# Two step orders of a two-layer mixture-of-experts kernel: MLA preparation steps in attention, and the last pair of experts

## The reference, cut to what matters

```
q_a = (rms_norm(q_lat, q_norm) @ w_uq).reshape(b, t, H_A, NOPE_A + ROPE_A)   # 8 heads, 64 + 32
kv  = (ckv @ w_ukv).reshape(b, t, H_A, NOPE_A + V_A)                         # keys 64, values 64
k   = concatenate([kv[..., :NOPE_A], broadcast(kpe)])
out = concatenate([o_mla, o_gqa]) @ w_out
```

```
hid = silu(einsum("nd,edf->nef", x, w_gate)) * einsum("nd,edf->nef", x, w_up)
y   = einsum("nef,efd->nd", hid * gates[:, :, None], w_down)
x   = layer_norm(ALPHA * x + mod_gate * y)
```

## Time and profile before

| what | before |
|---|---|
| median of 3 runs | 821.88 us (820.93 to 823.96) |
| the profiled execution's own time | 821.88 us |
| its span, first to last instruction | 820.1 us |
| TensorE matmuls busy | 759.0 us, 93% |
| VectorE, ScalarE, GpSimd busy | 237.2, 150.9, 59.7 us |
| read from memory | 278.99 MB, mean 350 GB/s |
| mean granted TensorE clock | 0.977 |

### The profile page before, as it was taken

The page is one execution under the profiler, slowest core; times in us unless marked ns, Lnnn a source line. Parts: engine busy times, 40 slices in busy tenths (PEclk is TensorE's granted clock), DMA queues, the critical chain, the costliest instruction groups (busy, mean ns, idle before and its releaser), DMA issues.

```text
span 820.1 us, 9612 instructions
## 1 busy us (share of the span) xinstructions
PE 759.0 (93%) x3769; PEld 361.2 (44%) x3769; DVE 237.2 (29%) x550; ACT 150.9 (18%) x390; POOL 59.7 (7%) x116
## 2 busy tenths in 40 slices
PE   4799799999999999997999999999999999997894
PEld 1345444556544443443334564455544434442431
DVE  0002634447401101000418227374601010010417
ACT  0110312325011110111112132233211101110200
POOL 0000000000100010101000110000100002101000
PEclk9599999999999999999999999999999999999998
DMA  8999999915399999999999999752299999999981
GB/s 305 390 304 396 390 390 416 415 68 206 121 418 417 419 421 417 419 416 415 421 401 374 389 380 423 299 211 104 109 419 416 422 417 416 421 418 416 418 352 52
DMA packets 78530, 287.46 MB, mean 351 GB/s; under 512 B 6508, under 2 KB 12140, under 8 KB 62100
## 3 DMA queue, kind: packets, MB, share of 16 engines
q1 hardware_dynamic: 74452, 275.60, 84.9%
q10 hardware_dynamic: 2880, 7.03, 2.2%
q0 software_dynamic: 1152, 4.19, 1.3%
HBM read 278.99 MB, written 7.82 MB: 350 GB/s over the span
## 4 chain that ended last, share of the span: by engine, by line
PE 56%; SPq 23%; DMA 9%; DVE 8%; ACT 3%; issue 2%; POOL 0%; DVEq 0%; ACTq 0%
PE bank L1094 13%; SPq L600 12%; PE bank L1128 7%; DMA ring<-in_exp_w_down 6%; SPq L595 6%; PE bank L932 6%; PE bank L789 5%; PE bank L769 4%; SPq L596 4%; PE bank L1065 3%; DMA ring<-in_w_mod 2%; PE bank L878 2%; PE bank L671 2%; PE bank L720 2%; PE bank L820 2%
## 5 line engine op out<-in xcount | busy, mean ns | idle before, releaser
L1094 PE MATMUL bank<-ring,arena 128*64 128x512 f32 x1024 | 227.6, 600 | 11.3 <-DMA ring<-in_exp_w_up 10.5
L1094 PEld LDWEIGHTS bank<-ring,arena 128*64 128x64 f32 x1024 | 75.2, 138 | 160.3 <-issue 148.8
L1128 PE MATMUL bank<-ring,arena 128*64 128x512 f32 x512 | 114.3, 596 | 6.0 <-DMA ring<-in_exp_w_down 4.9
L1679 DVE TENSOR_TENSOR arena<-bank,arena 128x256 f32<-128x256 f32 x32 | 13.6, 424 | 231.5 <-ACT arena L1848 231.5
L1128 PEld LDWEIGHTS bank<-ring,arena 128*64 128x64 f32 x512 | 35.8, 137 | 72.7 <-issue 63.6
L1065 PE MATMUL bank<-arena 128*128 128x128 f32 x512 | 62.1, 275 | 0.0
L1065 PEld LDWEIGHTS bank<-arena 128*128 128x128 f32 x512 | 59.7, 192 | 1.0 <-issue 0.5
L1758 ACT ACTIVATE arena<-bank 128x512 f32<-128x512 f32 (+6 forms) x67 | 37.2, 579 | 107.6 <-PE bank L789 34.0
L1848 ACT ACTIVATE arena<-bank 128x256 f32<-128x256 f32 x32 | 12.3, 383 | 225.7 <-PE bank L1094 225.7
L1695 DVE COPY arena<-bank 128x512 f32<-128x512 f32 x14 | 9.7, 691 | 118.7 <-PE bank L1128 118.7
L789 PE MATMUL bank<-ring,arena 128*128 128x256 f32 (+1 forms) x128 | 41.6, 486 | 0.0
(11 more groups left out here) (182 smaller groups left out, 679.6 us busy)
## 6 DMA issues: line engine op xcount, KB each, us to landing
ring<-in_exp_w_gate SPq DMA_DIRECT2D x64, 1024.0 KB, 19.8
ring<-in_exp_w_up SPq DMA_DIRECT2D x64, 1024.0 KB, 19.6
ring<-in_exp_w_down SPq DMA_DIRECT2D x64, 1024.0 KB, 23.7
ring<-in_w_mod SPq DMA_DIRECT2D x24, 2048.0 KB, 19.8
expert_rows<-arena ACTq DMA_DIRECT2D x12, 512.0 KB, 7.9
ring<-in_w_out_ab SPq DMA_DIRECT2D x2, 2048.0 KB, 19.2
ring<-in_w_in_c SPq DMA_DIRECT2D x2, 2048.0 KB, 23.2
ring<-in_w_out_c SPq DMA_DIRECT2D x2, 2048.0 KB, 12.0
```

The source lines that it names most:

```text
L1094: mm = nc.tensor.matmul(pb(key)[SLOTS * hf:SLOTS * (hf + 1), :], xeT[b][:, k * P + SLOTS * a:k * P + SLOTS * (a + 1)], w[:, :, k % 4, hf * ...
L1128: mm = nc.tensor.matmul(pb(key)[SLOTS * a:SLOTS * (a + 1), :], hp[:, c:c + SLOTS], w[:, a, kf % 2, hf * HALF:(hf + 1) * HALF], start=(kf = ...
```

## The change

The MLA preparation steps of layer 0 stand in another order and at other units (`make`), the turned queries of group 3 leave `between`, and the banks of `kn` and `qa` change: `kn` block 0 has bank 6 and block 1 bank 7 (before: bank 7, but bank 6 for group 2's block 1), `qa` of groups 0 and 1 has bank 7 (before: 6). In the last pair of experts TensorE does the first expert's gate and up before the one-hots and gates, and both halves of the spreading of pair 6's rows behind the first expert's turned hidden rows; VectorE takes the first hidden half before the returned rows; ScalarE's sigmoid of the first expert goes ahead of the copies of one-hots and gates.

```diff
@@ attention_steps
-    make = {0: [("qa", 0), ("kn", 0, 0)], 1: [("va", 0), ("qaT", 0)], 2: [("qa", 1), ("kn", 1, 0)],
-            3: [("va", 1), ("qaT", 1)], 4: [("qa", 2), ("kn", 2, 0)], 5: [("kn", 2, 1), ("qaT", 2)],
-            6: [("va", 2), ("kn", 3, 0)], 7: [("qa", 3), ("kn", 3, 1)], 8: [("va", 3)]}
-    between = {0: {1: [("me", 1)], 3: [("me", 2)], 5: [("me", 3)], 8: [("qaT", 3)],
-                   11: [("mt", 0)]},
+    make = {0: [("kn", 0, 0), ("qa", 0)], 1: [("qaT", 0), ("va", 0)],
+            2: [("kn", 1, 0), ("qa", 1)], 3: [("qaT", 1), ("va", 1)],
+            4: [("kn", 2, 0), ("kn", 2, 1), ("qa", 2)], 5: [("qaT", 2)],
+            6: [("va", 2), ("kn", 3, 0), ("kn", 3, 1), ("qa", 3)], 7: [("qaT", 3), ("va", 3)]}
+    between = {0: {1: [("me", 1)], 3: [("me", 2)], 5: [("me", 3)], 11: [("mt", 0)]},
@@ plan_turns
                     elif name == "kn":
-                        t.use(step, 6 if step[1:] == (2, 1) else 7)
+                        t.use(step, 6 + step[2])
                     elif name in ("qa", "qaT"):
-                        t.use(step, 6 if name == "qa" else 7)
+                        t.use(step, 6 if name == "qa" and u >= 2 else 7)
@@ TensorE, last_pair
                     pe.wait_ge(*saved(("xe", l, a), p))
+                gate_up(l, 0, n, None, p, p % 3, n - 2)
                 turn_onehots(l)
                 gates(l, 1)
-                pe.wait_ge(*saved(("ohT", l)))
-                pe.wait_ge(*saved(("ye", l, 0), p - 1))
-                spread(l, 0, ye_sb, 0, False)
-                gate_up(l, 0, n, None, p, p % 3, n - 2)
                 gate_up(l, 1, n + 2, None, p, p % 3, n + 1)
                 hidden_turned(l, 0, p, n + 3)
-                pe.wait_ge(*saved(("ye", l, 1), p - 1))
-                spread(l, 1, ye_sb, 0, False)
+                pe.wait_ge(*saved(("ohT", l)))
+                for hf in range(2):
+                    pe.wait_ge(*saved(("ye", l, hf), p - 1))
+                    spread(l, hf, ye_sb, 0, False)
                 hidden_turned(l, 1, p)
@@ VectorE, experts
+                both_hidden(l, N_PAIR - 1, (0,))
                 rows_taken(l)
-                both_hidden(l, N_PAIR - 1, (0,))
@@ ScalarE, last_pair
+                gate_exp(l, 0, p)
                 copy_out(("ohT", l), ohT)
                 gates(l, 1)
-                gate_exp(l, 0, p)
```

## The result

| | before | after |
|---|---|---|
| median of eight runs each, same chip | 822.19 us (820.5 to 824.5) | 828.94 us (827.9 to 832.1) |
| ratio, with its 95% interval | | 1.0093 (1.0074 to 1.0112) |
| the profiled execution's own time | 821.88 us | 832.93 us |
| its span | 820.1 us | 831.0 us |
| TensorE matmuls busy | 759.0 us | 760.6 us (92%) |

A forecast was written before the change was run, and what follows sets the result against it. TensorE's in-order list bounds attention, the weight stream the experts, and a delay in layer 0's attention moves the stream one for one. 2.24 + 2.28 + 2.49 = 7.01 on 821.88 gives 828.9 us, range 824.0 to 832.0.

The forecast's parts named there:

- Attention, 2.24 predicted: Layer 0's attention: TensorE's new bank waits, less those removed, make it 2.24 us later; bounds 2.8 gain to 5.2 loss.
- D: How late TensorE is in layer 0's attention; it reaches 5.31 us in unit 6 and stays at 2.24 from unit 8.
- T6: Turning of probabilities in unit 5: loses a key step and a wait of 1.41 ahead, 2.43 us earlier, leaving 1.37 late.
- T7: Turning of probabilities in unit 6, behind values, keys and queries in bank 6: 3.94 us later, making 5.31 late.
- rule on banks: Skill's rule that independent matmul groups rotate through PSUM banks; by it unit 6 is the costly place, unit 5 the gainer.
- Last pair, 2.28 and 2.49 predicted: Last pair of experts: TensorE waits 1.5 and 1.6 us for two blocks; loss 2.28 us in layer 0, 2.49 in layer 1.
- even landings: Weight stream in the last pair: 2 MB blocks land evenly, 5.06 us apart in layer 0 and 5.01 in layer 1.
- cover 0.6: Layer 0's last pair: VectorE's returned rows end at 418.9, 0.6 us before the second hidden half can start.
- Blocks already there: Last pair: gate and up halves land ahead of even spacing, so change 2 costs nothing: 824.1 us, chance 0.09.
- Attention gains: Layer 0's attention: copies leave bank 6 before TensorE asks, so change 1 is -2.8 us: 823.9 us, chance 0.09.
- Faster: Layer 0's attention: reordering removes two thirds (6.7 us) of TensorE's 10 us idle: 820.0 us, chance 0.04.
- Clock: Last pairs: TensorE's clock falls in the new waits, 1.7 us more per layer: up to 832.3 us, chance 0.12.

The follow-up runs named there:

- short loads: Kernel before and the last pair's new order, each loading only 128 of 2048 columns for the last pair's first two blocks in both layers: 823.41 and 823.58 us.
- another order of the same steps: Kernel before with two key steps ahead of the first values step in idle banks 3 and 2, group 3's queries a unit earlier: 819.55 us, ratio 0.9975.
- units 6 to 8: Kernel before with only the changed order and banks of units 6 to 8 of layer 0's attention: 824.86 us, ratio 1.0016.

## Why the prediction was right, and where it was not

The mechanism was right in both places: bank waits in attention, landings in the last pair. The fit of the total to 0.1 us was not earned, as the spread of the runs above shows.

**Attention, 2.24 predicted, 2.41 measured.** Lateness D against V0, predicted and measured: modulation of unit 0 0.55 and 0.40; of unit 2 1.13 and 1.18; of unit 4 3.80 and 3.98; T6 1.37 and 1.26; T7 5.31 and 5.61; output projection after T8 4.05 and 4.27; T9 2.24 and 2.46. The drains were named with their engines and nearly their sizes: 1.13 for ScalarE and 0.65 for VectorE in unit 4, 0.79 and 0.65 in unit 6. The one step overlooked is V6: it waits 0.40 for ScalarE's copy of the turned queries of group 2 in bank 7. A step's bank was checked for T, which the change touched, and not for V, whose neighbour changed. One reading was loose: of the waits called agreement with the rule on banks, 0.57 to 1.41, the one of 0.57 is a wait for the rotated queries and not for a bank.

**Last pair, 2.28 and 2.49 predicted, 2.31 and 2.69 measured.** The even landings held: TensorE's blocks 1 and 2 start at 402.85 and 407.73, and the last block of pair 6 at 397.80, so 5.05 and 4.88 apart where 5.06 was used. The waits were 1.39 and 1.23 where 1.5 and 1.6 were named. The second is shorter by 0.4 because the block's matmuls take 3.65 where 3.43 was used and the block lands 0.2 earlier. The loss in layer 1 is 0.2 larger than predicted. That layer 0 fits better is in part luck: the sum starts from before's own profile, whose last pair there was 0.25 slower than in the six other profiles of that order. The short loads exclude the other readings: without the landings to wait for, neither the spread's new place nor VectorE's new order costs anything.

**VectorE's move, cover 0.6 predicted, 1.12 measured** in layer 0, counted as in the prediction to the start of the second hidden half. That it is free held. Without TensorE's new order it costs 2.6, as the rows moved alone showed in layer 1.

**The sum**, 7.01 predicted, 7.41 by stages in the profile, 7.6 by the ratio of the means, 6.75 by the difference of the medians of eight. The stages are the measure to trust: in the second profile of the kernel after they give 7.44.

**Rivals.** Blocks already there: wrong, both waits are there; the short loads show what it would have been. Attention gains: wrong by the stage. Faster: wrong for this change, though another order of the same steps did gain 3.66 there. Clock: wrong at the place it was given. In the two profiles of the kernel after and the one of the last pair alone, all six last pairs have waits of 1.39 to 1.43 and 1.20 to 1.23 and then full-speed matmuls of 3.65. But it was right that a fall of the clock on the path moves the time: it did in attention (5.10 against 2.40 and 2.64, the second profile of attention alone) and in layer 0 with VectorE's rows alone moved (2.57). The prediction kept the clock's price for one place; it should have been a term on every run's start and routing stages. The range of 824 to 832 held the median, but its upper end was added up wrongly: the forecast with attention's upper bound (+3.0) and one clock fall (+1.7) is 833.6. Three of the fourteen runs lie between 832.0 and that, at 832.1 to 832.9.

**Open.** Half of the runs of attention alone are 5 to 6 us longer at a lower mean clock, and the fourteen runs of the kernel after fall into 826.9 to 829.1 (six) and 830.7 to 832.9 (eight) likewise. No such run of attention alone was profiled, so where its time goes isn't shown. Two runs of upper groups were profiled in other kernels: 832.93 of the kernel after has +0.94 ahead of V0, +1.19 in layer 0's routing and +1.58 in layer 1's over the 829.29, and 825.17 of units 6 to 8 has +2.75 ahead of V0 over before's profile. So the start and the routings are where to look first. None of the 53 runs of the kernel before beside the experiments had a mean clock under 0.971, where six of twelve of attention alone had 0.965 to 0.967. Whether the new order makes such runs more frequent isn't shown.

## What to carry to other kernels

Work that needs no new weights was free here ahead of a block that had not landed. Before dependent work is put ahead of it, work out the landing times from the spacing of earlier blocks and compare them with the time at which the block will be asked for. In an engine's in-order list, a step waits for the copy of the step before it in its bank, wherever that copy stands on the copying engine; so on changing a bank or a place, look at both neighbours of every step in both banks, and put steps into banks that are idle and times in which the engine waits anyway. A move that is free beside one change can cost 2.6 us without it: test the parts one by one. When executions of one kernel differ by more than the change, cut two profiles at common instructions and compare stage by stage.

## What the runs showed of the hardware that was not expected

- The same wait of 1.55 us for VectorE in layer 1's routing was followed by a granted clock of 1.00 in one profile and 0.54 in another. Waits of 1.2 to 1.4 us amid long matmuls were followed by full speed in all six last pairs of the new order; a wait of 2.63 was followed by 0.50 and one of 2.90 by 0.57, but one of 2.61 by full speed. In pair 6 of the kernel after a block's matmuls took 5.35 instead of 3.65 us behind waits of 2.23 and 2.28, and in its second profile 3.65 behind one of 2.26.
- One such fall made 9.66 us of 7.09 us of down projection. Where the stream set the pace it cost nothing, as in pair 6 of the kernel before.
- TensorE took up the first two blocks of 2 MB of layer 0's last pair 5.05 and 4.88 us after the block before them in the kernel after, and 5.04 and 4.88 us in that of the last pair alone, waiting for each. The memory stream ran at 420 GB/s over 398 to 405 us of the kernel after.
